# Four projection slabs of a two-layer decoder trunk in a wide matmul form, and the vector work around them

## Time and profile before

| | |
|---|---|
| median of 3 runs | 579.33 us |
| the profiled execution | 579.65 us, of which the span is 577.9 us |
| PE busy | 568.4 us (98%) |
| DVE busy | 440.4 us (76%) |
| ACT busy | 399.4 us (69%) |
| POOL busy | 64.5 us (11%) |
| mean DMA rate | 171 GB/s |

### The profile page before, as it was taken

How to read it: one execution, slowest core, us unless ns; L and a number is a source line. 1 busy time by engine, 2 the same in 40 slices (tenths; PEclk the granted TensorE clock), 3 DMA queues, 4 the chain that set the end, 5 groups by cost and what they waited for, 6 DMA issues and landing times.

```text
span 577.9 us, 8691 instructions
## 1 busy us (share of the span) xinstructions
PE 568.4 (98%) x3280; PEld 498.6 (86%) x3280; DVE 440.4 (76%) x699; ACT 399.4 (69%) x614; POOL 64.5 (11%) x75
## 2 busy tenths in 40 slices
PE   7999999999999999999999999999999999999995
PEld 6899888888888888888888889999889988888984
DVE  6889599788848874568767886799997974876763
ACT  6677795696657575557767858969659838566764
POOL 4002003039101000100000001111110100100002
PEclk9999999999999999999999999999999999999998
DMA  9756456556943544564446455326544563356202
GB/s 296 229 171 216 157 186 187 177 162 192 285 161 99 196 146 146 189 229 165 145 146 202 164 174 205 123 89 245 186 146 147 182 242 136 115 203 228 97 1 73
DMA packets 53133, 98.82 MB, mean 171 GB/s; under 512 B 1860, under 2 KB 8548, under 8 KB 53092
## 3 DMA queue, kind: packets, MB, share of 16 engines
q1 hardware_dynamic: 51908, 96.95, 49.6%
q0 software_dynamic: 1024, 1.05, 0.8%
q10 hardware_dynamic: 160, 0.27, 0.1%
HBM read 96.16 MB, written 1.05 MB: 168 GB/s over the span
## 4 chain that ended last, share of the span: by engine, by line
PE 97%; DMA 1%; DVE 1%; ACT 0%; issue 0%; DVEq 0%; SPq 0%; ACTq 0%
PE proj L2141 22%; PE proj L2142 11%; PE proj L2165 10%; PE proj L2166 10%; PE proj L2167 10%; PE proj L2124 5%; PE proj L2126 5%; PE proj L2125 5%; PE head L2371 4%; PE proj L2146 3%; PE proj L2145 2%; PE proj L2273 1%; PE head L2225 1%; DMA x_residual<-in_x_dram 1%; PE proj L2281 1%; PE head L2348 1%
## 5 line engine op out<-in xcount | busy, mean ns | idle before, releaser
L1267 DVE TENSOR_TENSOR w_lo<-raw_weights,w_hi 128x1024 fp32r<-128x1024 f32 x174 | 219.3, 1274 | 74.7 <-ACT w_hi L571 70.5
L571 ACT ACTIVATE w_hi<-raw_weights 128x1024 fp32r<-128x1024 f32 x174 | 181.7, 1056 | 94.7 <-PE proj L2167 48.1
L2141 PE MATMUL proj<-xT,w_hi 128*128 128x512 f32 x476 | 171.8, 400 | 0.0
L2142 PE MATMUL proj<-xT,w_lo 128*128 128x256 f32 x476 | 133.4, 280 | 0.0
L2141 PEld LDWEIGHTS proj<-xT,w_hi 128*128 128x128 f32 x476 | 89.5, 188 | 18.7
L2142 PEld LDWEIGHTS proj<-xT,w_lo 128*128 128x128 f32 x476 | 89.9, 189 | 2.2
L2165 PE MATMUL proj<-w_hi,y 128*128 128x512 f32 x176 | 69.1, 392 | 0.0
L2166 PE MATMUL proj<-w_hi,y 128*128 128x512 f32 x176 | 68.5, 389 | 0.0
L2167 PE MATMUL proj<-w_lo,y 128*128 128x512 f32 x176 | 68.5, 389 | 0.0
L2124 PE MATMUL proj<-xT,w_hi 128*128 128x256 f32 x224 | 64.1, 286 | 0.0
L2125 PE MATMUL proj<-xT,w_hi 128*128 128x256 f32 x224 | 63.4, 283 | 0.0
(11 more groups left out here) (338 smaller groups left out, 943.6 us busy)
## 6 DMA issues: line engine op xcount, KB each, us to landing
raw_weights<-in_ev_w_in_dram SPq DMA_DIRECT2D x13, 2048.0 KB, 9.0
raw_weights<-in_od_w_in_dram SPq DMA_DIRECT2D x12, 2048.0 KB, 8.0
raw_weights<-in_ev_w_out_dram SPq DMA_DIRECT2D x4, 2048.0 KB, 8.1
raw_weights<-in_xa_wkv_dram SPq DMA_DIRECT2D x4, 2048.0 KB, 7.7
raw_weights<-in_od_w_out_dram SPq DMA_DIRECT2D x4, 2048.0 KB, 8.0
raw_weights<-in_xa_wq_dram SPq DMA_DIRECT2D x2, 2048.0 KB, 8.9
raw_weights<-in_xa_wo_dram SPq DMA_DIRECT2D x2, 2048.0 KB, 8.6
raw_weights<-in_ev_w_in_dram SPq DMA_DIRECT2D x6, 512.0 KB, 7.3
```

Source lines behind the costliest of these rows:

```text
L571: act.activation(ring_quarter(w_hi, n, q), raw_quarter(n, q), ACT.Copy).then_inc(hi_ready, 1)
L1267: dve.tensor_tensor(ring_quarter(w_lo, n, q), raw_quarter(n, q), ring_quarter(w_hi, n, q).bitcast(F32), ALU.subtract).then_inc(lo_ready, 1)
L2141: pe.matmul(both, wh[:, k, :], x[:, :, k, :], start=(k == 0), stop=False)
L2142: pe.matmul(dst[:, 0:S], wl[:, k, :], x[:, 0, k, :], start=False, stop=False)
```

## The change

```diff
-    SLABS += [("D", "q", "F", _g), ("D", "k", "F", _g), ("D", "v", "T", _g), ("D", "z", "X", _g)]
+    SLABS += [("D", "q", "XX"[_g], _g), ("D", "k", "XX"[_g], _g), ("D", "v", "T", _g), ("D", "z", "X", _g)]
```

The four slabs q and k of D0 and D1 go from F to X (`D_WIDE` lists them). Each half is then copied by ACT (the first function) and summed by DVE (the second), and the rotation reads the sums:

```diff
+            def half_copied(n, w, u):
+
+                if n in D_WIDE:
+                    filled(act, n, 1, u)
+                    act.activation(blocks(w)[:, 2 * u:2 * u + 2, :], bank_halves(n, u, 0), ACT.Copy).then_inc(d_copied, 1)
...
+            def half_summed(n, w, u):
+
+                if n in D_WIDE:
+                    dve.wait_ge(d_copied, 2 * D_WIDE.index(n) + u + 1)
+                    rows = blocks(w)[:, 2 * u:2 * u + 2, :]
+                    dve.tensor_tensor(rows, bank_halves(n, u, 1), rows, ALU.add).then_inc(d_summed, 1)
+                    halves_freed(n, u)
```

On POOL, `decay_square` (both) and `conv_high` go to ACT, and `y_low(6)` goes to DVE as `gated_low(6)`:

```diff
             gated_input(0)
-            decay_square(0)
             gated_input(1)
-            conv_high()
-            decay_square(1)
-            for i in range(5, 8):
-                y_low(i)
+            y_low(5)
+            y_low(7)
```

On ACT, stage C1 and stage D:

```diff
                 z_half(z, 0)
                 if g:
+                    decay_square(0)
                     root_c(0)
                 ahead(z, 3)
+                if g:
+                    z_half(z, 1)
                 gate(g, 0)
...
             def stage_d(g):
                 ahead(q, 0)
-                z_half(slab("D", "z", 0) if g else slab("C", "z", 1), 1)
...
+                half_copied(q, 0, 0)
                 ahead(q, 2)
-                swap_halves(q, 0)
+                swap_halves(q, 0, 0)
                 ahead(q, 3)
+                half_copied(q, 0, 1)
                 ahead(k, 0)
-                swap_halves(q, 1)
+                swap_halves(q, 0, 1)
...
+                half_copied(k, 1, 0)
                 ahead(k, 2)
...
                 ahead(k, 3)
...
+                else:
+                    decay_square(1)
+                half_copied(k, 1, 1)
...
                 ahead(z, 0)
+                if g == 0:
+                    conv_high()
...
                 if g == 0:
+                    z_half(z, 1)
                     act.preload_act_table_set("natural_log_exp_and_others")
```

```diff
+            if n == slab("D", "z", 0):
+                return rope_tmp
             return zs[:]
...
+                if n == slab("D", "z", 0):
+                    act.wait_ge(k_ready, 4)
-                if i and SLABS[n][0] != "C":
+                elif i and SLABS[n][0] != "C":
```

The sums of the z slab of D0 are kept in `rope_tmp` rather than in `zs`, so that its `z_half` waits for the rotated keys (`k_ready`) rather than for the gated rows of C1 (`y_ready`). On DVE:

```diff
                 dve.tensor_tensor(wview(4), wview(4), wview(3), ALU.mult).then_inc(root_used, 1)
+                if g == 0:
+                    sum_z(slab("C", "z", 1), 1)
...
                 ahead(q, 0)
-                sum_z(slab("D", "z", 0) if g else slab("C", "z", 1), 1)
+                if g:
+                    dve.wait_ge(conv_hi_ready, 1)
+                    dve.tensor_tensor(y_lo[:, 0:4, :], y_src(4), y_hi[:, 0:4, :].bitcast(F32), ALU.subtract
+                                      ).then_inc(y_lo_ready, 1)
                 ahead(q, 1)
                 if g:
                     gated_d(0)
+                half_summed(q, 0, 0)
                 ahead(q, 2)
                 rope_full(q, 0, 0, q_ready, 4 * g + 1)
+                half_summed(q, 0, 1)
                 ahead(q, 3)
                 ahead(k, 0)
+                if g:
+                    gated_low(6)
                 ahead(k, 1)
+                half_summed(k, 1, 0)
                 rope_full(q, 1, 0, q_ready, 4 * g + 2)
                 ahead(k, 2)
                 rope_full(k, 0, 1, k_ready, 4 * g + 3)
                 ahead(k, 3)
+                half_summed(k, 1, 1)
                 if g == 0:
                     one_minus_a2(1)
                 ahead(v, 0)
                 rope_full(k, 1, 1, k_ready, 4 * g + 4)
...
                 decayed(g, (0, 1, 2, 3))
-                if g == 0:
-                    gated_c(1)
                 ahead(z, 1)
-                ahead(z, 2)
-                sum_z(z, 0)
-                if g == 0:
+                if g == 0:
+                    sum_z(z, 0)
+                    gated_c(1)
+                    ahead(z, 2)
                     square_low(2)
+                    sum_z(z, 1)
+                else:
+                    ahead(z, 2)
+                    sum_z(z, 0)
                 ahead(z, 3)
```

More of the change, by code:

```diff
@@ L68 @@
 Z_SLABS = [n for n, s in enumerate(SLABS) if s[1] == "z"]
+D_WIDE = [n for n, s in enumerate(SLABS) if s[0] == "D" and s[1] in "qk" and s[2] == "X"]
 def slab(stage, part, g=0):
@@ L170, in hybrid_trunk @@
         a_squared = sem("a_squared")
+        input_gated = sem("input_gated")
         mem_landed = sem("mem_landed")
@@ L277, in hybrid_trunk @@
         halves_swapped = sem("halves_swapped")
+        d_copied = sem("d_half_copied")
+        d_summed = sem("d_summed")
         early_ms = sem("early_ms")
@@ L505, in gated_input @@
                 pool.wait_ge(igate_ready, g + 1)
[L506 to L517, removed]
+                pool.tensor_tensor(blocks(4), blocks(4), conv_out(g), ALU.mult).then_inc(input_gated, 1)
             def mem_placed(t):
@@ L1070, in tanhs, with decay_square, conv_high @@
                 for h in range(4):
-                    last = act.activation(blocks(3)[:, h, :], blocks(3)[:, h, :], ACT.Tanh,
-                                          scale=soft[:, 6, 4 * g + h:4 * g + h + 1])
-                last.then_inc(decay_ready, 1)
+                    act.activation(blocks(3)[:, h, :], blocks(3)[:, h, :], ACT.Tanh,
+                                   scale=soft[:, 6, 4 * g + h:4 * g + h + 1])
+                act.drain().then_inc(decay_ready, 1)
+            def decay_square(g):
+                act.wait_ge(input_gated, g + 1)
+                act.activation(conv_out(g), blocks(5), ACT.Square).then_inc(a_squared, 1)
+            def conv_high():
+                act.wait_ge(y_ready, 5)
+                act.activation(y_hi[:, 0:4, :], y_src(4), ACT.Copy).then_inc(conv_hi_ready, 1)
             def root_c(g):
@@ L1149, in rstd_d, with swap_halves @@
                 act.activation(wview(4), wview(4), ACT.Exp, scale=-0.5).then_inc(o_rstd, 1)
-            def swap_halves(n, u):
-                filled(act, n, u)
+            def half_copied(n, w, u):
+                if n in D_WIDE:
+                    filled(act, n, 1, u)
+                    act.activation(blocks(w)[:, 2 * u:2 * u + 2, :], bank_halves(n, u, 0), ACT.Copy).then_inc(d_copied, 1)
+            def swap_halves(n, w, u):
+                wide = n in D_WIDE
+                if wide:
+                    act.wait_ge(d_summed, 2 * D_WIDE.index(n) + u + 1)
+                else:
+                    filled(act, n, u)
                 for a, b in ((0, 64), (64, 0)):
-                    last = act.activation(rope_tmp[a:a + 64, 2 * u:2 * u + 2, :],
-                                          bank(n, u)[b:b + 64, :].rearrange("p (h t) -> p h t", h=2), ACT.Copy)
+                    src = (blocks(w)[b:b + 64, 2 * u:2 * u + 2, :] if wide else
+                           bank(n, u)[b:b + 64, :].rearrange("p (h t) -> p h t", h=2))
+                    last = act.activation(rope_tmp[a:a + 64, 2 * u:2 * u + 2, :], src, ACT.Copy)
                 last.then_inc(halves_swapped, 1)
@@ L1966, in stage_c, with gated_low @@
                     gated_c(0)
+            def gated_low(i):
+                G = i % 4
+                dve.wait_ge(y_hi_ready, i + 2)
+                dve.wait_ge(y_lo_ready, i + 2)
+                dve.tensor_tensor(y_lo[:, 4 * G:4 * G + 4, :], y_src(i), y_hi[:, 4 * G:4 * G + 4, :].bitcast(F32),
+                                  ALU.subtract).then_inc(y_lo_ready, 1)
+            def half_summed(n, w, u):
[4 more added lines that the diff above has]
+                    halves_freed(n, u)
             def rope_full(n, u, w, done, i):
+                wide = n in D_WIDE
                 dve.wait_ge(halves_swapped, i)
-                src = bank(n, u)[:].rearrange("p (h t) -> p h t", h=2)
                 dst = blocks(w)[:, 2 * u:2 * u + 2, :]
+                src = dst if wide else bank(n, u)[:].rearrange("p (h t) -> p h t", h=2)
                 tmp = rope_tmp[:, 2 * u:2 * u + 2, :]
@@ L1975, in rope_full @@
                 dve.tensor_tensor(tmp, tmp, trig[:, 1:2, :].broadcast_to([P, 2, S]), ALU.mult)
-                dve.drain().then_inc(free_of(n, u), 1)
+                if wide:
+                    dve.drain()
+                else:
+                    dve.drain().then_inc(free_of(n, u), 1)
                 dve.tensor_tensor(dst, dst, tmp, ALU.add).then_inc(done, 1)
@@ L2026, in stage_d @@
                                       ).then_inc(y_lo_ready, 1)
+                ahead(q, 1)
+                if g:
+                    dve.drain()
+                    gated_d(0)
+                half_summed(q, 0, 0)
+                ahead(q, 2)
+                rope_full(q, 0, 0, q_ready, 4 * g + 1)
+                half_summed(q, 0, 1)
                 ahead(q, 3)
                 ahead(k, 0)
```

(26 more changed lines are left out.)

8 lines of the change are left out of this document (2 added, 6 removed).

## The result

The changed kernel takes 581.51 us (median of 6 runs, 581.11 to 581.82), the kernel before 579.33 us in the same set. The ratio is 1.004, with a 95% interval of 1.0031 to 1.005: slower by 2.2 us, where 2.1 were forecast.

What follows compares the result with a forecast made beforehand. TensorE, 98% busy, was taken to bound the kernel. Stalls of 0.87 and 2.11 us, less 1.09 of stream, plus 0.2 for D0, gave +2.1 us: 581.4 us, in itself 580.3 to 582.4; overall range 578.9 to 582.8.

Steps and rivals of the forecast that it cites:

- What bounds it: C1 to D1: TensorE, busy 98%, sets the time; no stall there to win back, only a shorter stream.
- The wide slabs: q and k in D0 and D1: the shorter TensorE stream gains 0.60 and 0.50 us, together 1.10 us.
- C1 at nothing: C1, ahead of D0: the moved gate halves and decay square neither cost nor gain time.
- D0 at 0.2: D0: VectorE's extra half sums overfill its queue; cost between 0 and 0.9 us, taken as 0.2.
- First stall: D1's mean products: the moved gated_c(1) makes VectorE's last square_low late, so TensorE waits 0.87 us.
- Second stall: D1's k, first quarter: its bank is released late by a half sum behind gated_d(0), so TensorE waits 2.11 us.
- Nothing in the rest of D1: D1 past k: y_low(6) moves from GpSimd to VectorE, which is no later than before; no stall.
- The sum: C1 to D1: stalls less stream give +1.89 us, with 0.2 for D0 +2.1 us, so 581.4 us.
- The signs: Trace after: D0's q, k, v 11.3 us apart, two D1 waits, gated_c(1) ending near 430; low-half waits mean too low.
- the first: Rival, whole stretch: everything is hidden and the full 1.1 us is gained, 578.2 us; chance 0.12.
- The second: Rival, D1: the wait at the mean products comes but the bank wait at k does not, 579.1 us; chance 0.15.
- The third: Rival, D0 and D1: VectorE overrun, 0.9 us in D0 and as much again in D1, 583.0 us; chance 0.15.

Runs made afterwards that it cites:

- e7: The changed kernel with q and k of D0 and D1 all in narrow slabs, only the moves of order left: 579.75 us, ratio 1.0015.
- e8: The kernel before with only both decay squares moved from GpSimd to ScalarE: 578.74 against 579.09 us, ratio 0.9994.
- e3: The changed kernel with ScalarE's copy of D0's first half of k ahead of the decays: 581.12 us, ratio 1.0031.
- e9: e5 plus, in D0 on VectorE, the last low half of v made ahead of one_minus_a2(1): 578.21 against 579.11 us, ratio 0.9988.
- e1: The changed kernel with gated_c(1) put back directly behind D0's mask products: 579.16 against 579.09 us, ratio 1.0001.
- e10: The changed kernel as it is, run again in a second set: 581.60 us against 579.11 for the kernel before, ratio 1.0039.
- e5: The changed kernel with gated_c(1) back, D1's first half of q summed ahead of gated_d(0), and e3's reordering: 578.38 us, ratio 0.999.
- e11: e9 with the subtraction y_low(5) on VectorE in D1 instead of GpSimd: 579.24 against 578.98 us, ratio 1.0007.

## Why the prediction was right, point by point

- **What bounds it.** Right in the main: each wait of TensorE is one of the whole. One thing besides the stream could be won, the 0.36 us of C1 below. The sum over the stretch, +2.59 us, is the time's +2.2 and +2.5 within their spread.
- **The wide slabs.** -1.1 us forecast. D0 gave 0.45 of 0.60 (0.55 against e7, which has the same order and narrow slabs), the four q quarters of D1 the 0.23 forecast, and k of D1 0.13 of 0.26 (446.00 to 457.39 is 11.39): 0.8 to 0.9 us in all. That is nearer to the 1.1 of the trace's pitches than to the 0.3 that the prediction works out by the Trainium skill (TensorE: Matmul & The Clock Gate, section "Back-to-back issue gap"). What is missing lies in the first quarter of q in D0 (2.96 us, the others 2.79 to 2.83) and of k in D1 (2.93 us).
- **C1 at nothing.** Mis-sized: it gave 0.36 us, 0.27 of it for good. Rows 3 held it, as gates of 3.63 us, and I did not ask what ended them (e8).
- **D0 at 0.2.** The size was off and the argument wrong. Measured 1.01 us (11.92 against 10.91), above the bound of 0.9. I reckoned VectorE overfull by its busy time. That sum also held 1.1 us which the change itself takes away: in the trace before, a conversion lasts 2.29 instead of 1.23 us while GpSimd's second square runs:

```profile
405.05 2.03 POOL L512 TENSOR_TENSOR v_rows<-work 128x1024 f32<-128x1024 f32 x1 [12.55 <-ACT work L1071]
405.87 2.29 DVE L1267 TENSOR_TENSOR w_lo<-raw_weights,w_hi 128x1024 fp32r<-128x1024 f32 x1 [0.55 <-ACT w_hi L571]
```

  The same stretches as in the earlier trace rows, after:

```profile
392.00:404.00 12.00, 12.00 (x68) 10.41 (x67) 9.12 (x12) 11.51 (x18) 0.00 (x0) 1.00 0.63 228
404.00:415.00 11.00, 10.63 (x45) 8.03 (x45) 10.61 (x15) 10.44 (x14) 0.00 (x0) 1.00 0.27 85
```

  VectorE (fourth figure) is busy 19.7 us, less than the 21.7 before, though TensorE waits. It stood idle before a half sum, for a copy that ScalarE makes behind the decays, and was late only then:

```profile
401.18 0.69 DVE L2009 TENSOR_TENSOR work<-proj,work 128x512 f32<-128x512 f32 x1 [2.26 <-ACT work L1162]
```

  e3 and e9 show it by order alone: 11.92, 11.30, 10.88 us, with the same work.
- **First stall, 0.87 us.** Measured 4.77 - 3.78 = 0.99, plus the 0.05 by which the wide quarter is shorter: 1.04. Cause as said (e1, e7).
- **Second stall, 2.11 us.** Measured 1.74 (TensorE was ready for k at 435.81 + 8.45 = 444.26, and k started at 446.00). The mechanism is as said. Counted from the gates, TensorE was ready 0.97 us later than reckoned and the release came 0.60 us later. D0 and C1 moved both by 0.80 us, because the chain starts in D0's z slab, so they do not change the stall. What made it shorter is that the first stall delayed TensorE 0.17 us more than reckoned, and that the chain itself was 0.20 us shorter.
- **Nothing in the rest of D1.** Right: 30.07 us as before.
- **The sum.** 0.36 too little gain in C1, 0.8 too little loss in D0, 0.17 too little at the first stall, some 0.3 too much gain in the stream and 0.4 too much loss at the bank. By the table that leaves 2.6 us for 2.1. The total came out close partly because these errors cancel, and the first set's 2.2 us happens to lie nearer to it than the 2.5 of e10's set. Both are luck.
- **The signs.** Those that the prediction named came, with D0's q, k and v 11.3 us apart (22.67 / 2). So did the one that it gave for a forecast too low: a wait for a low half stands in TensorE's list, 0.2 us at 411.78.

Of the rivals, the first (all hidden, 578.2 us or 1.1 of gain) is what e5 and e9 come half way to, by order, and with the help of the squares (e8); it is not what the change does. The second had the bank stall absent, and it was there. The third had D0's share right in size, 0.9 us, but not its cause, and its second wait in D1 did not come.

## What to carry to other kernels

When a form of a product is made cheaper but needs its banks back sooner, follow the bank's release back through the queues before counting the gain. And when a long chain (here gates, squares, roots, norm) begins with a call, moving that call 3 us back moves everything behind it, however little the engines are used. Look for idle time before the late instruction, not at the sum of busy time: three or four reorderings turned 2.2 us of loss into 0.6 to 0.9 of gain over the kernel before, with the work unchanged. And test the side moves by themselves: the squares off GpSimd alone (e8) gave about half of that gain.

## What the runs showed of the hardware

GpSimd at work can hold up a VectorE instruction. In e9 GpSimd subtracts 128x1024 from 428.62 to 431.03, and a conversion that VectorE starts at 429.42 takes 2.69 instead of 1.23 us, so that it ends 1.08 us behind GpSimd's end. Two conversions in the kernel before end just as far behind a product of GpSimd: at 391.60 behind 390.52, and at 408.16 behind 407.08. In the same kernel GpSimd multiplies 128x1024 from 371.43 to 373.37, and the first TENSOR_SCALAR of a pair, begun at 371.71, takes 1.81 us where the others of its form take 0.41, and ends at 373.52. The equal distance of 1.08 us speaks for a wait until GpSimd's instruction ends rather than for a slower pace.

The Trainium skill (SBUF — State Buffer, section "Who interferes with whom") says that a VectorE instruction with two SBUF inputs contends with a GpSimd instruction that reads SBUF. The conversion has two SBUF inputs, and its 2.69 us agree. For VectorE's modes that use two ports, the same section says that whichever engine issues first has the shared ports for the whole instruction while the other is blocked. The TENSOR_SCALAR reads one tensor, and its 1.81 us would agree with that, but no run here shows in which mode it ran.

e11 shows that taking the work off GpSimd pays only where VectorE has a place for it.
